# Every second addition to the residual on GpSimd, behind both output projections and at the end

## The reference

```
for l in range(DEPTH):
    h = rmsnorm(x, norm_g[l, 0])
    out = mixer(h)                      # ends with an output projection
    x = x + rmsnorm(out, norm_g[l, 1])
    h = rmsnorm(x, norm_g[l, 2])
    x = x + rmsnorm(swiglu(h, w_gate, w_up, w_down), norm_g[l, 3])
```

## Time and profile before

| | |
|---|---|
| median of 3 timed runs | 3450.28 us (3449.16 to 3450.61) |
| the profiled execution, as a run | 3448.8 us |
| its span in the trace | 3447.1 us |
| TensorE matmuls busy | 3161.2 us (92%) |
| VectorE busy | 1346.1 us (39%) |
| ScalarE busy | 871.7 us (25%) |
| GpSimd busy | 1119.4 us (32%) |
| mean granted clock of TensorE | 0.955 of full speed |

### The profile page before, as it was taken

One profiled execution on the slowest core, in us unless ns is written; L12 is line 12 of the kernel. 1 busy time (PEld: TensorE's weight loads), 2 busy tenths in 40 slices (PEclk: granted clock), 3 DMA queues, 4 the chain that ended last, 5 costly groups with the idle time before them and its releaser, 6 DMA issues.

```text
span 3447.1 us, 70424 instructions
## 1 busy us (share of the span) xinstructions
PE 3161.2 (92%) x30156; PEld 2946.0 (85%) x30156; DVE 1346.1 (39%) x1602; ACT 871.7 (25%) x1365; POOL 1119.4 (32%) x790
## 2 busy tenths in 40 slices
PE   7999989889999999958999798888878999999996
PEld 7989757879999999947999677667777999999995
DVE  5033173152222222278222366688724222222225
ACT  4132353230101101035211255444423100100102
POOL 2332210322332332221323355556432233232331
PEclk9999998999999999978999799899989999999998
DMA  3353452211111111123323222212041121111111
GB/s 100 118 136 104 148 163 68 98 31 43 49 49 38 54 48 37 43 81 117 129 86 113 57 73 73 56 46 67 32 161 31 34 58 48 34 58 43 43 46 58
DMA packets 327880, 247.41 MB, mean 72 GB/s; under 512 B 34407, under 2 KB 302131, under 8 KB 326780
## 3 DMA queue, kind: packets, MB, share of 16 engines
q1 hardware_dynamic: 307754, 199.90, 20.0%
q10 hardware_dynamic: 19922, 44.51, 3.4%
HBM read 181.09 MB, written 62.91 MB: 71 GB/s over the span
## 4 chain that ended last, share of the span: by engine, by line
PE 78%; DVE 9%; issue 5%; ACT 4%; POOL 2%; DMA 1%; SPq 1%; ACTq 0%; DVEq 0%; POOLq 0%
PE PS L514 54%; PE PS L1177 7%; PE PS L2351 2%; PE PS L2356 1%; DVE act_lo L2079 1%; PE PS L1936 1%; PE PS L1498 1%; PE PS L1917 1%; PE PS L598 1%; PE PS L2418 1%; PE PS L2368 1%; PE PS L1576 1%; PE PS L603 1%; DVE hf L449 1%; ACT i_nc L2626 1%
## 5 line engine op out<-in xcount | busy, mean ns | idle before, releaser
L514 PE MATMUL PS<-act_hi,w_hi 128*128 128x344 f32 x2976 | 954.3, 321 | 39.4 <-DVE act_lo L1779 25.2
L514 PE MATMUL PS<-act_lo,w_hi 128*128 128x344 f32 x2976 | 950.5, 319 | 0.0
L514 PE MATMUL PS<-act_hi,w_lo 128*128 128x344 f32 x2976 | 950.0, 319 | 0.0
L495 POOL CAST w_hi<-w_raw 128x1024 fp32r<-128x1024 f32 (+2 forms) x252 | 221.5, 879 | 1815.2 <-PE PS L514 1268.5
L514 PEld LDWEIGHTS PS<-act_hi,w_hi 128*128 128x128 f32 x2976 | 560.4, 188 | 43.5 <-issue 31.2
L514 PEld LDWEIGHTS PS<-act_lo,w_hi 128*128 128x128 f32 x2976 | 560.5, 188 | 0.0
L514 PEld LDWEIGHTS PS<-act_hi,w_lo 128*128 128x128 f32 x2976 | 560.4, 188 | 0.0
L497 POOL TENSOR_TENSOR w_lo<-w_raw,w_hi 128x1024 fp32r<-128x1024 f32 (+2 forms) x252 | 508.0, 2016 | 20.2
L514 PE MATMUL PS<-hid_hi,w_hi 128*128 128x344 f32 x1056 | 337.3, 319 | 4.9 <-DVE hid_lo L659 4.9
L514 PE MATMUL PS<-hid_lo,w_hi 128*128 128x344 f32 x1056 | 338.1, 320 | 0.0
L514 PE MATMUL PS<-hid_hi,w_lo 128*128 128x344 f32 x1056 | 337.8, 320 | 0.0
(11 more groups left out here) (493 smaller groups left out, 4543.0 us busy)
## 6 DMA issues: line engine op xcount, KB each, us to landing
w_raw<-in_ffn_w_gate_dram SPq DMA_DIRECT2D x44, 512.0 KB, 3.8
w_raw<-in_ffn_w_up_dram SPq DMA_DIRECT2D x44, 512.0 KB, 3.8
w_raw<-in_ffn_w_down_dram SPq DMA_DIRECT2D x80, 256.0 KB, 2.8
proj<-stage ACTq DMA_DIRECT2D x24, 516.0 KB, 2.7
rw<-z_st ACTq DMA_DIRECT2D x24, 516.0 KB, 2.7
rw<-stage ACTq DMA_DIRECT2D x24, 516.0 KB, 2.7
w_raw<-in_hyb_w_in_dram SPq DMA_DIRECT2D x24, 512.0 KB, 3.9
oT<-mix SPq DMA_DIRECT2D x8, 1032.0 KB, 8.2
```

Of the source, the lines that this page charges most:

```text
L495: nc.gpsimd.tensor_copy(w_hi[:, u, 0:kts, :], w_raw[:, u, 0:kts, :]).then_inc(w_hi_done, 1)
L514: mm = nc.tensor.matmul(PS[:, 3 * u + c, 0:CH], w[:, u, kt, :], x[:, kt, CH * c:CH * c + CH], start=(kt == 0 and part == 0), stop=(kt == k ...
```

## The change

`add_split_vector` and the end's `add_normed_vector` are put together in `add_terms_vector`. VectorE makes all eight terms as before and the additions of tiles 0, 2, 4 and 6. `add_terms_gpsimd` makes those of tiles 1, 3, 5 and 7 on GpSimd: it waits for the tile's term (add_t) and for the addition before it (x_ready), so that x_ready still counts the tiles in order. It stands in `ffn_gpsimd` behind the splits of the first pair of weight tiles, and once more at the end of GpSimd's program. The loops of `ffn_gpsimd` are cut so that this place exists. Behind the first FFN (n = 3) nothing is changed.

```diff
-        def add_split_vector(dve, n, m, r):
+        def add_terms_vector(dve, n, m, also=lambda k: None, last=KT + 1):
             dve.wait_ge(rstd_ready, n + 1 + START)
             if n == 5:
                 dve.wait_ge(x_back, 16 + START)
-            for k in range(KT + 2):
+            for k in range(last):
                 if k < KT:
                     if k >= 2:
                         dve.wait_ge(x_ready, KT * m + k - 1 + START)
                     nc.vector.scalar_tensor_tensor(hf[:, k % 2, :], oT[:, k, :], gains[:, n, k:k + 1], rstd[:, :],
                                                    ALU.mult, ALU.mult).then_inc(add_t, 1)
-                if 1 <= k <= KT:
+                if 1 <= k <= KT and k % 2:
+                    if k >= 2:
+                        dve.wait_ge(x_ready, KT * m + k - 1 + START)
                     dve.wait_ge(add_t, KT * m + k + START)
                     nc.vector.tensor_tensor(xT[:, k - 1, :], xT[:, k - 1, :], hf[:, (k - 1) % 2, :], ALU.add).then_inc(x_ready, 1)
+                also(k)
+
+        def add_terms_gpsimd(pool, n, m):
+            if n == 5:
+                pool.wait_ge(x_back, 16 + START)
+            for k in range(1, KT, 2):
+                pool.wait_ge(add_t, KT * m + k + 1 + START)
+                pool.wait_ge(x_ready, KT * m + k + START)
+                nc.gpsimd.tensor_tensor(xT[:, k, :], xT[:, k, :], hf[:, k % 2, :], ALU.add).then_inc(x_ready, 1)
+
+        def add_split_vector(dve, n, m, r):
+            def rest(k):
                 if k >= 2:
                     dve.wait_ge(hi_ready, KT * r + k - 1 + START)
                     nc.vector.scalar_tensor_tensor(act_lo[:, k - 2, :], xT[:, k - 2, :], gains[:, n + 1, k - 2:k - 1],
                                                    act_hi[:, k - 2, :].bitcast(F32), ALU.mult, ALU.subtract).then_inc(act_ready, 1)
+            add_terms_vector(dve, n, m, rest, KT + 2)
...
-        def ffn_gpsimd(pool, l):
+        def ffn_gpsimd(pool, l, n, m):
...
+            splits(0, 0, 1, KT, 0)
+            add_terms_gpsimd(pool, n, m)
+            body(0, HG, 1)
+            with pool.Fori(1, HGROUPS) as g:
+                body(g, HG)
+            body(HGROUPS, HREST)
...
-            ffn_gpsimd(pool, 1)
+            ffn_gpsimd(pool, 1, 5, 2)
+            add_terms_gpsimd(pool, 7, 3)
...
-            add_normed_vector(dve, 7, 3)
+            add_terms_vector(dve, 7, 3)
```

More of the change, by code:

```diff
@@ L467, in add_split_vector @@
                                                    ALU.mult, ALU.mult).then_inc(add_t, 1)
-                if 1 <= k <= KT:
+                if 1 <= k <= KT and k % 2:
+                    if k >= 2:
+                        dve.wait_ge(x_ready, KT * m + k - 1 + START)
                     dve.wait_ge(add_t, KT * m + k + START)
-                    nc.vector.tensor_tensor(xT[:, k - 1, :], xT[:, k - 1, :], hf[:, (k - 1) % 2, :],
-                                            ALU.add).then_inc(x_ready, 1)
+                    nc.vector.tensor_tensor(xT[:, k - 1, :], xT[:, k - 1, :], hf[:, (k - 1) % 2, :], ALU.add).then_inc(x_ready, 1)
+                also(k)
[8 more added lines that the diff above has]
+            def rest(k):
                 if k >= 2:
@@ L575, in ffn_sync, with splits, body @@
             ffn_groups(sp, body)
-        def ffn_gpsimd(pool, l):
+        def ffn_gpsimd(pool, l, n, m):
             k0, k1 = plan[f"ffn{l}"]
[L580 to L585, removed]
+            def splits(g, first, count, kts, off):
+                with pool.Fori(first, count) as i:
+                    for u, k in ((0, k0), (1, k1)):
+                        split_w(pool, u, g * 8 + (i + (k + off)), kts, g * 16 + (2 * i + (k0 + k1 + 2 * off + u + 1)))
+            def body(g, n, first=0):
+                splits(g, first, n, KT, 0)
+                splits(g, 0, KT // 2, n, n)
+            splits(0, 0, 1, KT, 0)
[4 more added lines that the diff above has]
+            body(HGROUPS, HREST)
         def ffn_tensor(pe, l, r, norm):
@@ L2919, in _ @@
             split_pairs(pool, "out0", 4, KT)
-            ffn_gpsimd(pool, 0)
+            ffn_gpsimd(pool, 0, 1, 0)
             mixes_gpsimd(pool)
```

## The result

Timed on one chip in turns, the changed kernel takes 3453.93 us (median of 22 runs, 3445.47 to 3462.35) and the kernel before 3444.29 (22 runs, 3436.53 to 3455.08). The ratio is 1.0024, 95% interval 1.0016 to 1.0032: slower by 8.3 us, 5.5 to 11.0. (The two medians are 9.6 us apart; the ratio goes by all the runs.) The three runs that stood ahead of the prediction are among the 22 and lie 5 to 6 us above their median.

The account below looks back on a forecast made before the run. TensorE was taken to bound most of the span, with VectorE nearly level at the entries and alone at the end. Terms 3.0 + 3.0 + 4.8 less 0.1 gave +10.7 us, from 3450.28 to 3461.0 us, range 3456 to 3466.

Parts of the forecast that it names:

- (2): VectorE at an FFN entry: a turn with GpSimd costs 3.37 us, +1.03 per pair of tiles (8.13 for 7.10).
- (3): TensorE behind VectorE at each entry: long stretch starts +2.97 us later, say +3.0, of VectorE's 4.2.
- (5): End of kernel: 6.09 us per pair in place of 4.94, so TensorE's transposes come +4.8 us later.
- (4): Work queued behind the additions, GpSimd's weight splits and VectorE's gatings: nothing added.
- The clock in the gate: TensorE at the entries: gaps of 0.4 to 1.7 us between products, no fall of the granted clock from 1.00.
- A: All three places: engines work side by side, sum +0.9 us, 3451.2 us; chance 0.08.
- B: Entries: turns starve TensorE, its clock falls to 0.50, some 5 to 10 us for both, about 3469; chance 0.04.
- C: Only the end pays, TensorE's trail covering VectorE's whole 4.2 at entries: +4.8 us, 3455.1; chance 0.04.
- D: The change does not do what it says, VectorE keeps all additions: 3450.3 us; chance 0.02.
- The 115 ns: Wait after the port lock's release; a blocked VectorE instruction would end 1.4 us after GpSimd, 3.5 us more for twelve additions.

Follow-up runs that it names:

- e4_end_psum: Only the end's additions shared with GpSimd, entries as before, the end's rstd in PSUM instead of SBUF; ratio to the kernel before 1.0001 [0.9988, 1.0014].
- e7_end_apart: Kernel before with end's rstd in PSUM, terms in place, GpSimd adding tiles 0, 1, 2 during the terms, VectorE the rest afterwards; ratio 0.9990 [0.9981, 0.9999].
- e1_again: The changed kernel once more, unaltered, beside the kernel before; ratio 1.0024 [1.0013, 1.0035].
- e3_entries_only: The change with only the two FFN entries shared with GpSimd, the end as before; ratio to the kernel before 1.0012 [1.0001, 1.0023].
- e8_first_only: Only entries shared, GpSimd making just the addition of tile 1 in each, VectorE the other seven; 3447.63 us, one run (before: 3443.05).
- e9_last_only: Only entries shared, GpSimd making just the addition of tile 7 in each, VectorE the other seven; 3444.88 us, one run (before: 3443.05).
- e2: The change with only the end's additions shared with GpSimd, entries left to VectorE, loops still cut; ratio to the kernel before 1.0009 [0.9998, 1.0019].
- e5: Kernel before with the end's rstd in PSUM and the cut loops, no additions on GpSimd; ratio to the kernel before 0.9994 [0.9983, 1.0004].
- e6: Only the end shared, rstd in SBUF, terms written over oT so neither engine waits for the other's additions; ratio to the kernel before 1.0005 [0.9993, 1.0016].

## Why the prediction was right or wrong

**The level was wrong.** 3461.0 was foretold with 3456 to 3466, and 3453.93 was measured. The term that was mis-sized is the one that the sum starts from, the kernel before: the profiled run of 3448.8 us and 1.5 on top, which gives the median of the three runs shown, 3450.28. I took three runs as the level of the kernel. Over 22 runs it is 3444.29, 6.0 us lower. Of the 7.1 us by which the forecast is too high 6.0 come from this term and 1.1 from the difference (10.7 foretold, the medians 9.6 apart); without the 1.5 us alone it would still have been 3459.5. The 35 runs of the kernel before that stood beside e4_end_psum to e7_end_apart go from 3431.43 to 3453.42. The difference, put on the level of the 22 runs, is 3444.3 + 10.7 = 3455.0. The range of about ±5 was worked out for the difference alone and had no room for the level.

Where the level comes from can be seen in part. The change and e1_again are one program, and their spans differ by 14.9 us. Between the end of the first FFN's long stretch and the start of the second's they take 1212.19 and 1199.60 us, 12.6 of the 14.9, with entries alike within 0.02. Long runs tend to have a low mean granted clock of TensorE: of the 35 runs above, the four with a mean clock of 0.953 or 0.954 took 3447.56 to 3453.42 us, the nine with 0.959 to 0.961 took 3431.43 to 3441.49. In a stretch of the scan, 1930 to 2100 us, the granted clock (the third number from the end) differs too; the change, e1_again, e3_entries_only and before, in this order:

```profile
1930.00:2100.00 170.00, 139.35 (x3624) 109.18 (x3628) 93.61 (x141) 79.93 (x180) 85.88 (x63) 0.86 0.26 69
```

```profile
1930.00:2100.00 170.00, 141.24 (x3922) 113.51 (x3922) 102.16 (x150) 78.06 (x175) 86.90 (x63) 0.89 0.24 65
```

```profile
1930.00:2100.00 170.00, 142.16 (x3681) 113.64 (x3681) 93.54 (x141) 79.18 (x178) 85.44 (x62) 0.83 0.26 69
```

```profile
1930.00:2100.00 170.00, 137.13 (x3821) 109.75 (x3822) 102.26 (x148) 81.18 (x182) 88.27 (x64) 0.89 0.26 69
```

0.86 and 0.83 go with 1212.19 and 1209.46 us, 0.89 with 1199.60 and with 1202.93 before, whose second entry is 3.1 us shorter. But this one stretch does not explain the level: in e8_first_only and e9_last_only it has 0.84 and 0.86, and they take 1201.37 and 1200.67 us. Of the three profiles with four turns at both entries two have the longest times of layer 1 and one, e1_again, the shortest. That the clock is the cause of the longer runs was not tried, only seen together, and why it differs from run to run stays open.

**The difference was right in sign and mechanism.** Of the three pieces: (2) the turn of 2.27 + 1.10 measured 2.24 + 1.08, the pair 8.08 for 8.13. (3) an entry +2.97 measured +3.16 and +3.13. (5) the end +4.8 measured +4.56: GpSimd ends 2.22, not 2.27, behind the term, and three pairs are 6.01 us, not 6.09. The sum 10.7 measured 10.85 by the profiles, 8.3 (5.5 to 11.0) by the runs. (4) nothing behind the additions is late: GpSimd's next split starts when TensorE is through (749.36), VectorE's second gating still waits for TensorE (0.44 us, 1.36 before), the long stretches are unchanged. The clock in the gate did not fall again: from 725 to 749 us the granted clock is 1.00, and the last product takes 1.42 us as before.

**What was mis-sized in (3)** is the kernel before, not the one after. I took TensorE's start at an entry from two entries, 29.48 and 29.53. Where nothing is shared, the 12 entries of six profiles (before, e2, e4, e5, e6, e7) run from 29.48 to 30.65, 29.90 in the mean, the two of before among the four shortest, by when the clock rises. In the kernel before it is 1.00 from 5.4 and 5.9 us behind the first addition's end and TensorE's first product takes 1.42; in e2_end_only's first entry it is 8.3 and 2.52. Where all four turns are taken, the six entries are 32.64 to 32.67: VectorE carries the chain and hides when TensorE's clock rises. By this mean an entry costs 32.65 - 29.90 = 2.75 us, and the change 2 x 2.75 + 4.56 = 10.1, nearer to the middle of the interval. Five of the six profiles have the cut loops of the change and the kernel before has one profile alone. Entries with cut loops can be as short as its own (29.51, 29.52, 29.56), but that its own mean is 29.90 is not shown. With 29.90 the pieces still say 1.8 us more than the runs for the change, 1.4 for e3_entries_only, and 1.1 to 2.2 for e2, e4, e5 and e6; for e7 0.8 less. All of it is inside the intervals, and whether something else is given back stays open.

**The rivals.** A (side by side) fell by the rows of 724.68 and 3422.46, and e4_end_psum shows that its sum was right for operands that do not meet: 1.3 foretold, 1.45 measured. B (clock) was not seen. C (only the end pays) fell by e3_entries_only. D fell by the instruction counts. The 115 ns of the Trainium skill, SBUF — State Buffer, "A bandwidth-pool intuition that's wrong (but worth ruling out)", are stated for a DMA that waits; an estimate by them has a blocked VectorE instruction end 1.4 us behind GpSimd, and the trace does not agree: 1.08 and 1.09. By the Trainium skill, SBUF — State Buffer, "Who interferes with whom", a VectorE instruction with two SBUF inputs contends with a GpSimd instruction that reads SBUF, and one with at most one SBUF input, outside VectorE's 2-port modes, does not. The traces agree with both: with two the two engines took turns (3.40 us), with one, in e4_end_psum, VectorE kept 1.29 us and GpSimd 2.36.

## What to carry to other kernels

Work moved from VectorE to an idle GpSimd ran beside it here only where VectorE's instructions did not read two SBUF tensors: look for pairs in the trace in which one of the two is 1 to 2 us longer than usual, and count a turn as GpSimd's whole duration plus VectorE's less a little (2.24 + 1.08 us here, for 2.36 and 1.29 alone), not as zero. Putting one operand in PSUM may free the pair (e4_end_psum, e7_end_apart). And for a change of a few tenths of a per cent, foretell the difference from pieces of the trace, and give the level the spread of many runs, not of three.

## What was not expected of the hardware

The moment at which TensorE's granted clock goes up behind an idle stretch moves from entry to entry and between executions of one program. In all 22 entries of the eleven profiles TensorE had been idle for 8.2 us before its first sum, and the clock went from 0.50 to 1.00 3.1 to 6.0 us after that sum began; for the change and e1_again, one program, it was 6.0 and 4.0 us, then 3.9 and 4.2. In the unshared entries the start of tile 1's sum lies 7.25 to 8.58 us behind the first addition's end (chain of waits), and the whole entry moves with it (29.48 to 30.65).
